# A two-block transformer forward pass on one core: the first attention's scores scaled, masked and reduced in one VectorE instruction per token block, with its first division and the second query pair's transposes moved up

## The reference, cut to what matters

```python
def body(args):
    qn, qp, c = args
    logits = (jnp.einsum('bhqd,bhkd->bhqk', qn, k_nope)
              + jnp.einsum('bhqd,bkd->bhqk', qp, k_pe)).astype(jnp.float32) * scale
    q_idx = c * Q_BLOCK + jnp.arange(Q_BLOCK)
    causal = k_idx[None, :] <= q_idx[:, None]
    logits = jnp.where(causal, logits, -jnp.inf)
    p = jax.nn.softmax(logits, axis=-1).astype(v.dtype)
    return jnp.einsum('bhqk,bhkd->bhqd', p, v)
```

## Time and profile before

| | before |
|---|---|
| time, median of 3 runs | 895.45 us (895.38 to 895.51) |
| span of the profiled execution | 893.8 us |
| PE busy | 882.5 us, 99% of the span |
| VectorE busy | 633.2 us, 71% |
| ScalarE busy | 523.2 us, 59% |
| GpSimd busy | 41.0 us, 5% |
| DMA | 143.73 MB, mean 161 GB/s |

### The profile page before, as it was taken

One profiled execution on the slowest core, in us unless ns is written; L12 is line 12 of the kernel. 1 busy time (PEld: TensorE's weight loads), 2 busy tenths in 40 slices (PEclk: granted clock), 3 DMA queues, 4 the chain that ended last, 5 costly groups with the idle time before them and its releaser, 6 DMA issues.

```text
span 893.8 us, 13052 instructions
## 1 busy us (share of the span) xinstructions
PE 882.5 (99%) x5231; PEld 767.7 (86%) x5231; DVE 633.2 (71%) x1047; ACT 523.2 (59%) x855; POOL 41.0 (5%) x72
## 2 busy tenths in 40 slices
PE   9999999999999999999999999999999999999997
PEld 8888888888888888888888888999989998798885
DVE  6897876766575666567656556679899867767774
ACT  6998444453454577645444445466556756747782
POOL 0151000000000000000000000000014310000000
PEclk9999999999999999999999999999999999999999
DMA  8732545554644454447555655455251312654511
GB/s 305 232 111 62 209 161 209 184 176 160 247 171 166 165 176 150 144 133 249 185 188 170 217 193 174 146 187 161 78 187 48 111 55 56 228 212 142 188 48 47
DMA packets 60877, 143.73 MB, mean 161 GB/s; under 512 B 4497, under 2 KB 6673, under 8 KB 60817
## 3 DMA queue, kind: packets, MB, share of 16 engines
q1 hardware_dynamic: 60816, 142.91, 47.0%
HBM read 141.85 MB, written 1.05 MB: 160 GB/s over the span
## 4 chain that ended last, share of the span: by engine, by line
PE 94%; ACT 3%; DVE 2%; DMA 1%; issue 1%; SPq 0%; DVEq 0%
PE ps L509 89%; PE ps L517 5%; ACT arena L1440 1%; DMA raw<-mla_w_in_dram 1%; ACT xhl L1440 0%; ACT whi L1440 0%; DVE arena_r L2426 0%; DVE sub L2426 0%; DVE arena L2426 0%; DVE wlo L2426 0%; DVE X L2432 0%; DVE st L2432 0%; ACT L1443 0%; ACT st L1440 0%; SPq L3810 0%
## 5 line engine op out<-in xcount | busy, mean ns | idle before, releaser
L2426 DVE TENSOR_TENSOR wlo<-raw,whi 128x2048 fp32r<-128x2048 f32 (+4 forms) x141 | 300.2, 2137 | 109.0 <-ACT whi L1440 108.8
L1440 ACT ACTIVATE whi<-raw 128x2048 fp32r<-128x2048 f32 (+6 forms) x143 | 251.8, 1771 | 165.1 <-PE ps L509 150.3
L509 PE MATMUL ps<-xhl,whi 128*128 128x512 f32 (+1 forms) x912 | 214.0, 348 | 0.0
L509 PE MATMUL ps<-whi,xhl 128*128 128x512 f32 (+2 forms) x528 | 167.2, 385 | 1.8 <-DVE xhl L2432 1.3
L509 PE MATMUL ps<-whi,oth 128*128 128x512 f32 x416 | 165.2, 397 | 0.0
L509 PEld LDWEIGHTS ps<-xhl,whi 128*128 128x128 f32 x912 | 149.8, 188 | 14.8 <-DVE xhl L2432 0.2
L509 PE MATMUL ps<-whi,otl 128*128 128x512 f32 x416 | 162.4, 390 | 0.0
L509 PE MATMUL ps<-wlo,oth 128*128 128x512 f32 x416 | 162.2, 390 | 0.0
L509 PE MATMUL ps<-xhl,wlo 128*128 128x256 f32 x704 | 135.6, 281 | 0.0
L509 PEld LDWEIGHTS ps<-xhl,wlo 128*128 128x128 f32 x704 | 115.2, 189 | 10.8
L509 PEld LDWEIGHTS ps<-whi,xhl 128*128 128x128 f32 x528 | 98.5, 189 | 20.1 <-issue 2.8
(11 more groups left out here) (146 smaller groups left out, 830.8 us busy)
## 6 DMA issues: line engine op xcount, KB each, us to landing
raw<-mlp_w_in_dram SPq DMA_DIRECT2D x32, 1024.0 KB, 5.3
raw<-mlp_w_out_dram SPq DMA_DIRECT2D x32, 1024.0 KB, 4.9
raw<-gdn_w_in_dram SPq DMA_DIRECT2D x16, 1024.0 KB, 5.3
raw<-moba_w_qkv_dram SPq DMA_DIRECT2D x12, 1024.0 KB, 5.3
raw<-kv_w_dram SPq DMA_DIRECT2D x8, 1024.0 KB, 5.5
raw<-fox_w_in_dram SPq DMA_DIRECT2D x8, 1024.0 KB, 5.1
raw<-mla_w_o_dram SPq DMA_DIRECT2D x4, 1024.0 KB, 5.8
raw<-moba_w_o_dram SPq DMA_DIRECT2D x4, 1024.0 KB, 6.1
```

The lines of the kernel that those rows point to most:

```text
L509: return eng.matmul(o, l, r, start=start, stop=True, skip_group_check=True)
L1440: return eng.activation(o, i, f, **kw)
L2426: return eng.tensor_tensor(o, a, b, f)
```

## The change

It has four parts.

1. `logits("mla", j)` was one `scalar_tensor_tensor` over 384 columns (scale, then mask) and two `reduce_max` over what it wrote. It is now two `tensor_tensor_reduce`, over 128 and 256 columns, each of which adds the mask, multiplies by -1/sqrt(192), writes, and takes the minimum. The exponential takes the sign back with `scale=-1`, and waits for `s_sx` in place of `s_mx`. `s_sx` is now signalled after both, and it is also what frees the bank of the scores. The other two attentions compute as before.
2. PE: `q_T(1)` moves ahead of `turn_p("mla", 0)`.
3. ACT: `divide("mla", 0)` moves ahead of `exp("mla", 1)`; `q_squares(2)` moves from ahead of `exp("mla", 0)` to behind `divide("mla", 1)`; `q_copy(1)` moves up to stand right behind `p_copy("mla", 0)`.
4. DVE: `q_sums(2)` moves from between the first two reciprocals to behind `k_norm(1)`.

```diff
@@ tensor_program
             to(9, 0)
             score_pair(0)
             to(10, 0)
+            q_T(1)
             turn_p("mla", 0)
             qp_T(1)
-            q_T(1)
             turn_p("mla", 1)
             value("mla", 0)
             value("mla", 1)
@@ scalar_program, exp
-                L.wait_ge(s_mx, J + 1)
+                if stage == "mla":
+                    L.wait_ge(s_sx, J + 1)
+                else:
+                    L.wait_ge(s_mx, J - 7)
...
-                act(Q[:, 0:128], S[:, 0:128], ACT.Exp, bias=ng[:, 0:1], accum_out=su[:, 0:1])
+                sign = -1.0 if stage == "mla" else 1.0
+                act(Q[:, 0:128], S[:, 0:128], ACT.Exp, bias=ng[:, 0:1], scale=sign, accum_out=su[:, 0:1])
@@ scalar_program
             hi(10)
-            q_squares(2)
             exp("mla", 0)
             k_copy(0, 1)
+            divide("mla", 0)
             exp("mla", 1)
-            divide("mla", 0)
             divide("mla", 1)
+            q_squares(2)
             p_copy("mla", 0)
+            q_copy(1)
             rsq("mla_k1")
             qp_copy(1)
             p_copy("mla", 1)
-            q_copy(1)
             uq_copy(3, 0)
             rsq("mla_q2")
             o_hi("mla", 0)
@@ vector_program, logits
-                    stt(S, b[:, 0:384], float(1.0 / np.sqrt(192.0)), K("mask"), ALU.mult, ALU.add).then_inc(s_sx, 1)
...
+                    for t, (c0, c1) in enumerate(((0, 128), (128, 384))):
+                        ins = eng.tensor_tensor_reduce(S[:, c0:c1], b[:, c0:c1], K("mask")[:, c0:c1], float(-1.0 / np.sqrt(192.0)),
+                                                       3.0e38, ALU.add, ALU.min, ng[:, t:t + 1])
+                    ins.then_inc(s_sx, 1)
+                    return
@@ vector_program
             over_sum("mla", 0)
-            q_sums(2)
             over_sum("mla", 1)
             lo(10)
             rsq_b("mla_k1")
             k_norm(1)
+            q_sums(2)
             rsq_b("mla_q2")
             o_lo("mla", 0)
```

More of the change, by code:

```diff
@@ L1548, in exp @@
                 S, Q = a.S[j % 2], a.Q[j % 3]
-                act(Q[:, 0:128], S[:, 0:128], ACT.Exp, bias=ng[:, 0:1], accum_out=su[:, 0:1])
-                act(Q[:, 128:384], S[:, 128:384], ACT.Exp, bias=ng[:, 1:2], accum_out=su[:, 1:2]).then_inc(s_ex, 1)
+                sign = -1.0 if stage == "mla" else 1.0
+                act(Q[:, 0:128], S[:, 0:128], ACT.Exp, bias=ng[:, 0:1], scale=sign, accum_out=su[:, 0:1])
+                act(Q[:, 128:384], S[:, 128:384], ACT.Exp, bias=ng[:, 1:2], scale=sign, accum_out=su[:, 1:2]).then_inc(s_ex, 1)
             def divide(stage, j):
@@ L2520, in logits @@
                     L.wait_ge(s_pr, 16)
-                    stt(S, b[:, 0:384], float(1.0 / np.sqrt(192.0)), K("mask"), ALU.mult, ALU.add).then_inc(s_sx, 1)
[L2522 to L2526, removed]
+                    for t, (c0, c1) in enumerate(((0, 128), (128, 384))):
[3 more added lines that the diff above has]
+                    return
+                bias = biasM[:, j, :] if stage == "moba" else bb[j % 4]
+                L.wait_ge(s_rq, (0 if stage == "moba" else 2) + j // 4 + 1)
+                stt(S[:, 0:128], b[:, 0:128], rq[stage][:, 0, j:j + 1], bias[:, 0:128], ALU.mult, ALU.add)
+                stt(S[:, 128:384], b[:, 128:384], rq[stage][:, 1, j:j + 1], bias[:, 128:384], ALU.mult, ALU.add).then_inc(s_sx, 1)
                 L.wait_ge(s_sx, J + 1)
```

## The result

The changed kernel takes **897.81 us** (median of 11 runs, 897.08 to 898.59) against 895.51 us for the kernel before (11 runs, 894.63 to 897.13): a ratio of 1.0024, 95% interval 1.0016 to 1.0031. It is 2.3 us slower. The forecast was 898.4 us, 0.6 us too high, with the right sign.

What follows compares the result with a forecast made beforehand. The prediction took TensorE, busy 882.5 of 893.8 us, as the bound. New waits for ACT and VectorE make PE 3.1 us late, 0.1 comes back: 895.45 + 3.0 = 898.4 us, range 897.2 to 900.8.

Steps and rivals of the forecast that it cites:

- the stall of 1.14 us: PE's one wait in the first attention before the change, ahead of turn_p(0), for ACT's first division; forecast to return larger, 0.72.
- No wait ahead of the first four transposes: On PE, q_T(1) starts at 54.54 and turn_p(0) behind it no longer waits for the first division.
- ACT idle of 0.41 ahead of exp(0), start 52.08: The first exponential waits for head 0's scores, done at 52.04, where q_squares(2) had filled the time.
- the lower bound of the prediction, 0.55: A head's scores on VectorE with the row results free: 0.55 us against 0.73 taken, for 898.1 us in all.
- ACT idle of 0.37 ahead of divide(1): The second division stands right behind its exponential and waits for the reciprocal, starting at 55.50.
- turn_p(1) waits 0.8, value(0) 1.4, start 58.1: PE waits for divide(1), then for bank 4, which q_T(1) holds until q_copy(1) is through at 58.01.
- rsq q2 waits 2.2 us, o_hi(0) at 61.96: ACT's square root waits for q_sums(2), now late on VectorE; o_hi(0) behind it starts three microseconds later.
- PE idle 0.9 and 0.8 ahead of k_T(1, 0) and q_T(2): PE waits for o_lo(0) to free bank 4, then for head 2's scores to free bank 6.
- PE 3.1 late, 0.1 back, 3.0 in all: PE reaches q_T(2) 3.1 us late, the shorter scores give 0.1 back later, and the span grows by 3.0.
- The rival of a falling clock: PE's stalls within 10 us halve its clock to 1.2 GHz, up to 6 us more, 904; chance 0.06.
- The rival of the dear instruction: The new score instruction takes 1.3 us a head or more on VectorE, 901; chance 0.10.
- That of the first half only: VectorE's chain for k1 and q2 isn't late; PE keeps 1.0 to 1.4 us at the values, 896.8; chance 0.08.

Runs made afterwards that it cites:

- e4: The changed kernel with 5 and 10 idle multiplications on PE in its two new stalls, before turn_p(1) and value(0); 898.60 us, ratio 1.0029.
- e5: The changed kernel with q_T(1) put back to its old place on PE, behind qp_T(1); 898.05 us, ratio 1.0027.
- e1: The changed kernel with the PE, ACT and DVE orders taken back, the new score instruction kept; 895.37 us, ratio 0.9997.
- e2: The changed kernel with the old three score instructions back, all new orders kept; 899.42 us, ratio 1.0040.
- e3: The changed kernel with q_sums(2) moved up on DVE, ahead of rsq_b(k1) and k_norm(1); 897.39 us, ratio 1.0014.
- e11: The same program as e3, run and profiled again on another chip; 897.57 us, ratio 1.0020.
- e6: The changed kernel with the ACT and DVE orders of before, so new scores and only q_T(1) early on PE; 896.62 us, ratio 1.0013.
- e10: e6 with 4 idle multiplications on PE before turn_p(0) and 10 before value(0); 896.82 us, ratio 1.0014.

## Why the prediction was right, and what it sized wrong

The forecast was that the stall of 1.14 us returns larger, behind `q_copy(1)` and `q_sums(2)`. Its rows in order, with 0.10 us added to those of the kernel after for its earlier start:

- *No wait ahead of the first four transposes*: as forecast.
- *ACT idle of 0.41 ahead of exp(0), start 52.08*: 51.94, so 0.27 us of idle. A head's scores take 0.56 us and not 0.73, since reading the row results is nearly free. This was the lower bound of the prediction, 0.55. The Trainium skill's rule ("VectorE: DVE Perf Modes", The DRAIN you can't avoid) would have given 1.05 by the prediction's estimate. But the same section says that a next operation that isn't held back starts earlier, which the prediction left out. The rows at 51.38 and 51.72, where a read and the next operation start together, agree with that. (The prediction puts the sum 0.5 us higher at 1.05; as each 0.1 us counts twice, it is 0.6, and its own 899.0 has that.)
- *ACT idle of 0.37 ahead of divide(1)*: 0.23.
- *turn_p(1) waits 0.8, value(0) 1.4, start 58.1*: 0.62 and 1.23, start 57.94.
- *rsq q2 waits 2.2 us, o_hi(0) at 61.96*: 2.05 us, 61.66. Of the 0.30 us, 0.23 had been there since `rsq_b(k1)`; from the start of `q_sums(2)` to the square root it is 61.20 - 59.88 = 1.32 and not 61.62 - 60.23 = 1.39.
- *PE idle 0.9 and 0.8 ahead of k_T(1, 0) and q_T(2)*: in the changed kernel neither shows, since the half clock fills them; at full clock (e4, e5) they are 0.92 and 0.42.
- *PE 3.1 late, 0.1 back, 3.0 in all*: 2.62 late, 0.32 back, 2.30 in all. The largest mis-sized term is the scores. They enter twice, 0.14 at the first exponential and 0.08 at the bank of `q_T(2)` (0.78 us from the start of the scores of head 2 in e4 and e5, for 64.80 - 63.94 = 0.86). Smaller ones of 0.02 to 0.08 us (from exp(0) to divide(1), from there to `rsq_b(k1)` and `q_sums(2)`, `q_sums(2)` itself, the step to the scores of head 2) make up the rest of the 0.5. And the give-back is three times what I took.

The working of the step behind the sum is confirmed from both sides: e1 has the instruction and no loss, e2 the orders and all of it. At full clock e3 takes out `q_sums(2)` and 1.41 us go; what remains there is stall ahead of `turn_p(1)` and `value(0)`. The waits for VectorE that the prediction gave are seen as such in e4 and e5 alone, and give 2.60 and 2.62.

The rival of a falling clock had 0.06 and "up to 6 us more". The clock did fall, in the very stretch, and the argument against it (it stayed at full through 1.14 us) was too weak: two stalls of 0.62 and 1.23 us with 1.15 and 0.55 us of transposes around them are another case than one. Yet it cost nothing on top here, and its price where it is bare is 1.46 us, a quarter of that bound. So the forecast of 3.0 us came near the 2.3 also by luck: a loss that it left out was hidden under a wait that it had counted. In the profiled execution the low clock alone would have given the same lag without that wait, as e11 shows with 2.67. The rival of the dear instruction is out. That of the first half only is out too: at full clock it would have looked like e3, and in e4 and e5 the second half is there.

## What to carry to other kernels

Before a step is moved into an engine's idle time, ask whose result that engine was waiting for, and which buffer the moved step will hold: here PE's early transpose took a bank that the next value product needed, and its release stood behind ACT's queue. A step with a round trip behind it (sum on DVE, square root on ACT, outputs queued behind) must not slip behind other work only because it isn't due next. And an instruction that is 0.6 us cheaper on an engine that others don't wait for at that point is worth what the first engine behind it can use. In the traces that was 0.3 us with the old orders (e1) and 0.8 with the new ones (2.30 us at the end against 3.11 in e2). And before a loss is put down to one cause, see whether a second stands behind it: here the low clock and the late `q_sums(2)` covered each other, and taking out either one alone gave nothing back.

## What the runs showed of the chip

- `tensor_tensor_reduce` over 128 and 256 columns from PSUM takes 287 and 419 ns, against 285 and 419 for a two-tensor operation without a reduction; the read of its row result is 83 ns and lies under the next operation.
- PE's granted clock fell to half for 3.4 us behind two stalls of 0.62 and 1.23 us, in one execution and not in another of the same program (e11 and e3, on two chips; the clocks listed for e3's own runs point to both on one chip). Where it wasn't hidden it cost 1.46 us, and 1.47 by e6 against its filled kernel e10. What decides whether it falls stays open.
- A stall and a low clock can replace each other in a trace with no change in the time: the kernel after and e5 have the same distance of 29.44 us, one with 3.4 us at half clock, the other with 1.34 us more of waits for VectorE.
